# The last down projection of a two-layer trunk: the activations become the stationary operand and the weights stream, with output rows summed in the PSUM banks

## The chip, the cores and the metric

The kernel runs on one core of one Trainium2 chip. The metric is the device time of one execution in microseconds; the time before is the median of three runs. Beside it stands one execution that the hardware profiler recorded, and all rows below come from that one. Its engines are called PE (TensorE, the matmuls), PEld (the loads of PE's stationary operand), DVE (VectorE), ACT (ScalarE), POOL (GpSimd) and SP (SyncE, which here only issues DMAs).

## The reference

One step of a two-layer trunk on 512 prompt tokens and 8 x 8 sample tokens, together T = 576 tokens, with model width 1024 and a hidden width of 2816. Each layer is a mixer (a causal pool and a convolution in layer 0, a gating MLP in layer 1), and then a gated ConvFFN; each adds to the residual x. At the end stands one more RMSNorm. What matters here is the end of the last layer:

```python
def rmsnorm(x, g):
    xf = x.astype(jnp.float32)
    y = xf * lax.rsqrt(jnp.mean(xf * xf, axis=-1, keepdims=True) + EPS)
    return (y * g.astype(jnp.float32)).astype(x.dtype)
...
        h = rmsnorm(x, p["ffn_norm"][layer])
        up = h @ p["w_up"][layer]
        c, fb = causal_dwconv(up, ffn_bufs[layer], p["ffn_conv_w"][layer], p["ffn_conv_b"][layer])
        x = x + (jax.nn.silu(c[..., :D_FF]) * c[..., D_FF:]) @ p["w_down"][layer]
        new_ffn.append(fb)
    y = rmsnorm(x, p["final_norm"])
```

## The kernel before, in words

**Layout.** The kernel keeps everything transposed: features on the 128 partitions, the 576 tokens along the free dimension. The residual `X` is eight such tiles (KD = 8). A product gives one tile of 128 output features: the weights are the stationary operand (128 x 128), the activations move.

**Precision.** Each operand is split in a high part (fp32r, made by ACT with a copy) and a low part (raw minus high, made by POOL for the weights, by DVE for the activations). Each product is three matmuls: high x high, high x low, low x high. The instructions that split weights are called `split_n` (L1041 on ACT, L1664 on POOL) and, for the last projection, `last_split` (L1511 on ACT, L1935 on POOL). The four slots `w_hi[0..3]` and `w_lo[0..3]` hold 1024 columns each; `weights_at` (L127) plans which half slot a unit uses and after which unit it is free.

**The FFN in groups.** The 22 hidden tiles come in groups of 6, 6, 6 and 4. For each group the up projections, the convolution and the gating are computed, then the down projection adds the group's share to the residual. The first three groups use a scheme with fewer products. The last group has 4 hidden tiles (nt = 4) and ends the kernel: its down projection is what the change touches. Its input is `gh`, `gl` (named last_group_hi and last_group_lo in the rows), its weights are 8 tiles of 128 x 512.

**The last stage before.** The tokens are cut in two parts (`LAST`, L256): first tokens 256 to 575 (320 columns), then tokens 0 to 255. For each part PE makes eight output tiles, so there are 16 steps n, each of 4 x 3 = 12 products into bank n % 4. Steps 0 to 3 are interleaved: nine products of each, then, once the last hidden tile is there (`h_lo_ready`), the last three of each. After a step, DVE adds the residual (L2583), ACT squares the sum (L1525), ACT multiplies it by the gain of the final norm (L1533, `gained`), DVE adds the squares up (L2592), PE turns the gained tile in 128 x 128 transposes to rows (L911, `out_rows`), and DVE copies the rows to `y_rows` (L2598). At the end of a part PE sums the squares over the partitions (L634, `row_sums`), ACT takes the root (L1560), DVE the reciprocal (L2605), and the rows are scaled: those of the first part by POOL (L1974), those of the second by DVE (L2628, L2631), ACT (L1636) and POOL (L1978) together. Four DMAs from SP (L572, L574, L576) and one from ACT (L1641), of one row block of up to 128 tokens each, write them.

**What sets the order.** Each engine runs its own list in the order written, and waits on semaphores by count: `lo_ready` (a weight tile is split), `h_lo_ready` (a hidden tile is split), `acc_free` (a bank has been read), `unit_done` (a unit's products are done). Nothing is reordered by a scheduler.

Of the kernel before, what the change touches and what calls it, by code (L numbers as in the profile page):

```python
# [25 lines left out]
F32 = mybir.dt.float32  # L26
# [4 lines left out]
P = 128  # L31
# [5 lines left out]
def hybrid_trunk(nc, x, params, w_in_ab, pool_w, w_out_ab, w_in_c, w_out_c, w_up, w_down, gate_w, gate_bias,  # L37
                 gate_w_samples, pool_state, conv_state, ffn_state, state_pool, state_conv, y_prompt, y_sample,
# [96 lines left out]
    def layer_weights(u0):  # L135

        half = 0
        for g, run in enumerate(RUNS):
# [11 lines left out]
            for n in range(MS if FAST[g] else KD):  # L150
                weights_at(ud + n, half + (HALF_OF[n] if FAST[g] else 2 * n), 1 if FAST[g] else 2)
# [104 lines left out]
    LAST = (((P * 2, T), range(2, RT)), ((0, P * 2), range(2)))  # L256
# [17 lines left out]
    with ExitStack() as ctx:  # L274
# [10 lines left out]
        w_hi = [sb(f"w_hi{s}", [P, KD * P], F32R) for s in range(4)]  # L285
        w_lo = [sb(f"w_lo{s}", [P, KD * P], F32R) for s in range(4)]
# [9 lines left out]
        std = sb("std", [P, RT])  # L296
        rinv = sb("rinv", [P, RT])
# [22 lines left out]
        def cut(start, *dims):  # L320
# [5 lines left out]
            if len(dims) == 2:  # L326
# [38 lines left out]
        KL = GROUPS[-1][1] * P  # L365
        last_hi, last_lo = ([w[m][:, :] for m in range(4)]
                            + [v[:, :, :].rearrange("p k t -> p (k t)")[:, m * KL:(m + 1) * KL] for m in range(4)] for w, v in ((w_hi, xh), (w_lo, xl)))
        xg = mem[:, 0:2 * T].rearrange("p (a b) -> p a b", a=2)
# [72 lines left out]
        y_row_done, y_left, y_right = sem("y_row_done"), sem("y_left"), sem("y_right")  # L441
        xg_last, y_turned = sem("xg_last"), sem("y_turned")
        xg_ready, y_T, yrow_ready, y_scaled, st_y = sem("xg_ready"), sem("y_T"), sem("yrow_ready"), sem("y_scaled"), sem("st_y")
# [63 lines left out]
        def _(sp):  # L507
# [40 lines left out]
            for layer in range(2):  # L548
# [5 lines left out]
                for g, (t0, n) in enumerate(GROUPS):  # L554
# [12 lines left out]
                    for m in range(KD):  # L567
                        load(R_FFN[layer] + R_DOWN[g] + m, w_down[layer, m, :, t0 * P:(t0 + n) * P])
            for n, r in enumerate(LAST[0][1]):
                sp.wait_ge(y_row_done, n + 1)  # L570
                if r < CH:
                    sp.dma_start(yp_rows[:, r, :], y_rows[:, r, :]).then_inc(st_y, 16)  # L572
                else:
                    sp.dma_start(ys_rows, y_rows[P - SM:P, CH, :]).then_inc(st_y, 16)  # L574
            sp.wait_ge(y_scaled, 2)
            sp.dma_start(yp_rows[:, 0, :], y_rows[:, 0, :]).then_inc(st_y, 16)  # L576
# [6 lines left out]
            sp.wait_ge(st_y, 16 * RT)  # L583
# [3 lines left out]
        def _(pe):  # L587
# [41 lines left out]

            def row_sums(src, first=True, final=True, bank=S0, at=0, rows=range(RT)):  # L630

                for r in rows:
                    lo = r * P if r < CH else T - P
                    last = nc.tensor.matmul(PS[:, bank, at + r:at + r + 1], src[:, lo:lo + P], ones[:, 0:1],  # L634
                                            start=(first and r == rows[0]), stop=(final and r == rows[-1]),
                                            skip_group_check=True)
                return last
# [266 lines left out]
            def out_rows(n):  # L904

                pe.wait_ge(*((xg_ready, n + 1) if n < 2 * KD - 1 else (xg_last, 1)))
                if n >= 2:
                    pe.wait_ge(yrow_ready, n - 1)
                for a, r in enumerate(LAST[n // KD][1]):
                    lo = r * P if r < CH else T - P  # L910
                    last = nc.tensor.transpose(PS[:, M0 + n % 2, a * P:(a + 1) * P], xg[:, n % 2, lo:lo + P], ident[:, :])  # L911
                last.then_inc(y_T, 1)

# [75 lines left out]

            def last_products(n, ks):  # L990

                m, (lo, hi) = n % KD, LAST[n // KD][0]
# [14 lines left out]
            for n in range(4, 2 * KD):  # L1007
                if n < KD:
                    pe.wait_ge(lo_ready, ud + n + 1)
                pe.wait_ge(acc_free, ud + n - 3)  # L1010
                last_products(n, range(nt // 2))
                for q in ((0, 1) if n == 4 else (2, 3) if n == 5 else (n - 2,)):
                    out_rows(q)
                if n == KD + 1:
                    pe.wait_ge(sq_added, (KD - 1) * 4 + KD - 2)
                    row_sums(sqacc, final=False, rows=LAST[0][1])
                    pe.wait_ge(sq_ready, KD * 5)
                    row_sums(sq[:, 1, :], first=False, rows=LAST[0][1]).then_inc(var_mm, 1)
# [1787 lines left out]
```

## Time and profile before

| | |
|---|---|
| time, median of 3 runs | 1164.09 us (1163.95 to 1164.12) |
| the profiled execution: its own time | 1163.62 us |
| the profiled execution: span of its instructions | 1161.9 us |
| PE busy | 1145.3 us, 99% of the span, 8442 matmuls |
| DVE / ACT / POOL busy | 818.0 / 580.0 / 722.1 us |
| granted clock of PE, mean over the span | 0.998 |

The span runs from the first to the last instruction; the execution's own time is 1.72 us longer. Busy times of PE overlap, since matmuls are pipelined: a matmul's row starts when the one before is still draining, so what one costs is the distance between starts, not its length. The share of busy time says that PE bounds nearly the whole of the kernel; the last 42 us, which the change rewrites, are to be read from their own rows.

### The profile page before, as it was taken

The page shows a single profiled execution, that of the slowest core. Times are in us where ns is not written, and L with a number is a line of the kernel's source. Part 1 is how long each engine was busy: PE and PEld are TensorE (multiplying, and loading weights), DVE is VectorE, ACT ScalarE, POOL GpSimd, SP SyncE. Part 2 cuts the span into 40 slices and gives each one's busy share as a digit, 9 for nine tenths or more (in the row PEclk, how much of TensorE's full clock was granted, in tenths as well). Part 3 has the DMA queues.
Part 4 walks back from the last instruction along what each step waited for, and adds up shares of the span by engine and source line. Part 5 has one row for each costly group of instructions (what it writes and reads, how often), then busy time and mean ns, then how long its engine had stood idle before and what let it go on. Part 6 is the DMA issues. An engine that isn't in the chain of part 4 may idle for free. (4 is left out here: it accounts for less than half of the span.)

```text
span 1161.9 us, 21843 instructions
## 1 busy us (share of the span) xinstructions
PE 1145.3 (99%) x8442; PEld 1124.9 (97%) x8442; DVE 818.0 (70%) x1506; ACT 580.0 (50%) x1113; POOL 722.1 (62%) x691
## 2 busy tenths in 40 slices
PE   8999999999999999999999999999999999999997
PEld 8887999999999999999999999999999999999997
DVE  5999768878677867775614644388686778678655
ACT  7475555544554555453613533366346545654543
POOL 3996344359867985872564324334698679768633
PEclk9999999999999999999999999999999999999999
DMA  6311242203421422131422222322042213232312
GB/s 233 117 56 36 67 146 81 93 28 95 142 65 44 149 73 92 56 137 51 149 84 91 69 69 74 117 82 65 28 147 91 80 61 116 74 92 80 120 51 82
DMA packets 35688, 104.01 MB, mean 90 GB/s; under 512 B 5105, under 2 KB 7153, under 8 KB 35569
## 3 DMA queue, kind: packets, MB, share of 16 engines
q1 hardware_dynamic: 31504, 98.92, 26.9%
q10 hardware_dynamic: 4080, 3.69, 1.1%
q8 instruction: 67, 1.10, 0.4%
q14 instruction: 37, 0.30, 0.1%
HBM read 98.29 MB, written 4.79 MB: 89 GB/s over the span
## 5 line engine op out<-in xcount | busy, mean ns | idle before, releaser
L594 PE MATMUL psum<-x_hi,w_hi 128*128 128x320 f32 (+2 forms) x1564 | 336.4, 297 | 1.3 <-POOL w_lo L1664 1.3
L594 PE MATMUL psum<-x_lo,w_hi 128*128 128x320 f32 (+2 forms) x1564 | 334.8, 295 | 0.0
L594 PE MATMUL psum<-x_hi,w_lo 128*128 128x320 f32 (+2 forms) x1564 | 334.1, 295 | 0.0
L1664 POOL TENSOR_TENSOR w_lo<-w_raw,w_hi 128x1024 fp32r<-128x1024 f32 (+1 forms) x84 | 181.8, 2169 | 188.0 <-ACT w_hi L1041 188.0
L594 PEld LDWEIGHTS psum<-x_hi,w_hi 128*128 128x128 f32 x1564 | 258.8, 188 | 3.6 <-POOL w_lo L1664 1.6
L594 PEld LDWEIGHTS psum<-x_hi,w_lo 128*128 128x128 f32 x1564 | 258.5, 188 | 0.0
L594 PEld LDWEIGHTS psum<-x_lo,w_hi 128*128 128x128 f32 x1564 | 257.3, 188 | 0.0
L2412 DVE SCALAR_TENSOR_TENSOR psum<-arena,params,psum 128x608 f32<-128x608 f32 x176 | 150.4, 854 | 58.8 <-ACT psum L1420 55.8
L1806 POOL TENSOR_TENSOR w_lo<-arena,w_hi 128x384 fp32r<-128x384 f32 x120 | 130.8, 1109 | 49.6 <-ACT w_hi L1331 49.6
L839 PE MATMUL psum<-block_hi,w_lo 128*128 128x288 f32 x504 | 149.2, 296 | 0.0
L839 PE MATMUL psum<-block_hi,w_hi 128*128 128x288 f32 x504 | 149.2, 296 | 0.0
L839 PE MATMUL psum<-block_lo,w_hi 128*128 128x288 f32 x504 | 149.1, 296 | 0.0
L1664 POOL TENSOR_TENSOR w_lo<-arena,w_hi 128x1024 fp32r<-128x1024 f32 (+1 forms) x49 | 111.4, 2290 | 47.5 <-ACT w_hi L1041 47.5
L1420 ACT ACTIVATE psum<-arena,params 128x608 f32<-128x608 f32 x88 | 75.9, 862 | 74.1 <-DVE arena L2065 57.4
L1041 ACT ACTIVATE w_hi<-w_raw 128x1024 fp32r<-128x1024 f32 (+1 forms) x84 | 78.2, 939 | 69.0 <-PE psum L594 48.8
L1331 ACT ACTIVATE w_hi<-arena 128x384 fp32r<-128x384 f32 x120 | 58.7, 518 | 87.7 <-DVE arena L2276 28.2
L839 PEld LDWEIGHTS psum<-block_hi,w_lo 128*128 128x128 f32 x504 | 95.0, 188 | 0.0
L839 PEld LDWEIGHTS psum<-block_lo,w_hi 128*128 128x128 f32 x504 | 94.9, 188 | 0.0
L839 PEld LDWEIGHTS psum<-block_hi,w_hi 128*128 128x128 f32 x504 | 94.9, 188 | 0.0
L2290 DVE TENSOR_TENSOR residual<-psum,residual 128x288 f32<-128x288 f32 x168 | 71.7, 452 | 22.4 <-ACT squares_sum L1370 12.9
L2291 DVE TENSOR_TENSOR block_lo<-psum,block_hi 128x288 fp32r<-128x288 f32 x144 | 56.6, 415 | 20.5 <-ACT block_hi L1397 7.9
L2058 DVE TENSOR_TENSOR arena<-psum,rstd 128x512 f32<-128x512 f32 x68 | 46.7, 687 | 31.5 <-PE psum L594 31.4
(270 smaller groups left out, 2207.1 us busy)
## 6 DMA issues: line engine op xcount, KB each, us to landing
w_raw<-in_w_up SPq DMA_DIRECT2D x44, 512.0 KB, 3.7
arena<-in_w_up SPq DMA_DIRECT2D x44, 512.0 KB, 4.3
arena<-in_w_down SPq DMA_DIRECT2D x24, 384.0 KB, 3.6
w_raw<-in_w_down SPq DMA_DIRECT2D x24, 384.0 KB, 3.2
w_raw<-in_w_in_c SPq DMA_DIRECT2D x16, 512.0 KB, 3.5
w_raw<-in_w_in_ab SPq DMA_DIRECT2D x11, 512.0 KB, 3.6
w_raw<-in_w_out_ab SPq DMA_DIRECT2D x16, 256.0 KB, 2.7
w_raw<-in_w_out_c SPq DMA_DIRECT2D x8, 512.0 KB, 3.6
```

The costliest lines, as they stand in the source:

```text
L594: last = nc.tensor.matmul(PS[:, 2 * (q % 2 if slot is None else slot) + half, 0:b - a], w[q][:, k * P:(k + 1) * P], r[:, r_at, a:b], start ...
L839: last = nc.tensor.matmul(PS[:, BANK[n], 0:HALF], ws[w][:, cols + k * P:cols + (k + 1) * P], rs[:, block, k, :], start=(k == 0 and a == 0) ...
L1041: nc.scalar.activation(w_hi[slot][:, 0:nk * P], raws[RAW_SLOT[raw]][:, 0:nk * P], ACT.Copy).then_inc(hi_ready, 1)
L1331: nc.scalar.activation(w_hi[HALF_AT[ud + n] // 2][:, at:at + nk * P], src, ACT.Copy).then_inc(hi_ready, 1)
L1420: nc.scalar.activation(conv_acc(j), window(j, 0), ACT.Identity, bias=pcol("ffn_conv_b", ti + layer * 2 * KF), scale=pcol("ffn_conv_w", ti ...
L1664: nc.gpsimd.tensor_tensor(w_lo[slot][:, 0:nk * P], raws[RAW_SLOT[RAW[u]]][:, 0:nk * P], w_hi[slot][:, 0:nk * P].bitcast(F32), ALU.subtract ...
L1806: nc.gpsimd.tensor_tensor(w_lo[w][:, at:at + nk * P], src, w_hi[w][:, at:at + nk * P].bitcast(F32), ALU.subtract).then_inc(lo_ready, 1)
L2058: nc.vector.tensor_tensor(halves(dst[:, pad:pad + PR]), PS[:, 2 * slot:2 * slot + 2, 0:cut], halves(rstd[:, 0:PR]), ALU.mult)
L2290: plus = lambda out, a, b: nc.vector.tensor_tensor(out, a, b, ALU.add)
L2291: minus = lambda out, a, b: nc.vector.tensor_tensor(out, a, b, ALU.subtract)
L2412: nc.vector.scalar_tensor_tensor(out=conv_acc(j), in0=window(j, k), scalar=pcol("ffn_conv_w", ti + (layer * FK + k) * 2 * KF), in1=conv_ac ...
```

## The change

The last down projection is turned around. The activations (128 hidden features x up to 128 tokens) are the stationary operand, and the weights move, 512 columns (four output tiles) at a time. The output has tokens on the partitions, as it is to be stored. The steps are now 10: five row blocks (four of 128 prompt tokens, one of the 64 sample tokens), for the left 512 output features, and then the same five for the right. Each step begins with four transposes of the residual into the bank, and the 12 products are added on top. ACT squares the bank and sums along the row in the same instruction (`accum_out`), DVE multiplies by the gain, which now lies along the row and is loaded by one more DMA (L570 of the new kernel), and by the reciprocal root. The steps that added the residual, gained, turned back and copied are gone, and so is POOL's scaling.

For the weights to stream in one access pattern over four tiles, they all lie in `w_hi` and `w_lo` as half slots: the planner gives each of the eight tiles one half (before, the first four took a whole slot each and the others lay in the space of `x_hi`, `x_lo`). The order of the splits is unchanged on both engines.

```diff
             for n in range(MS if FAST[g] else KD):
-                weights_at(ud + n, half + (HALF_OF[n] if FAST[g] else 2 * n), 1 if FAST[g] else 2)
+                if not FAST[g] and u0 == U_FFN1:
+                    weights_at(ud + n, half + n, 1)
+                else:
+                    weights_at(ud + n, half + (HALF_OF[n] if FAST[g] else 2 * n), 1 if FAST[g] else 2)
...
-    LAST = (((P * 2, T), range(2, RT)), ((0, P * 2), range(2)))
+    LAST = [(r, h) for h in range(2) for r in range(RT)]
...
+                        if layer == 1 and g == len(GROUPS) - 1 and m == KD // 2:
+                            sp.wait_ge(unit_done, U_FFN1 + U_PAIR[RUNS[g][-1]])
+                            sp.dma_start(gain_row, final_gain.to_broadcast([P, D])).then_inc(ld_gain, 16)
...
+            for r in range(CH):
+                sp.wait_ge(y_row_done, r + 1)
+                sp.dma_start(yp_rows[:, r, :], y_rows[:, r, :]).then_inc(st_y, 16)
+            sp.wait_ge(acc_free, N_UNITS - KD + 2 * RT)
+            sp.dma_start(ys_rows[:, D // 2:D], y_rows[0:SM, CH, D // 2:D]).then_inc(st_y, 16)
...
+            def residual_rows(n):
+
+                tokens, rows, tiles = rows_of(n)
+                for a, m in enumerate(range(KD)[tiles]):
+                    nc.tensor.matmul(PS[0:rows, n % 4, a * P:(a + 1) * P], X[:, m, tokens], ident[:, :], start=(a == 0), stop=False,
+                                     is_transpose=True, skip_group_check=True)
...
-                    for a, (ws, rs) in enumerate(((last_hi, gh), (last_hi, gl), (last_lo, gh))):
-                        last = nc.tensor.matmul(PS[:, n % 4, 0:hi - lo], ws[m][:, k * P:(k + 1) * P], rs[:, k, lo:hi],
-                                                start=(k == 0 and a == 0), stop=(k == nt - 1 and a == 2))
+                    for a, (ws, rs) in enumerate(((hi_all, gh), (hi_all, gl), (lo_all, gh))):
+                        last = nc.tensor.matmul(out, rs[:, k, tokens], halves_of(ws)[:, :, k * P:(k + 1) * P],
+                                                start=False, stop=(k == nt - 1 and a == 2), skip_group_check=True)
...
             for n in range(4):
-                pe.wait_ge(lo_ready, ud + n + 1)
                 pe.wait_ge(acc_free, ud - 1 + n // 2)
-                pe.wait_ge(h_lo_ready, H_FFN[1] + nt - 1)
+                residual_rows(n)
+            pe.wait_ge(lo_ready, ud + KD // 2)
+            pe.wait_ge(h_lo_ready, H_FFN[1] + nt - 1)
+            for n in range(4):
                 last_products(n, range(nt - 1))
             pe.wait_ge(h_lo_ready, H_FFN[1] + nt)
             for n in range(4):
                 last_products(n, [nt - 1]).then_inc(unit_done, 1)
...
+            for n in range(4, 2 * RT):
                 pe.wait_ge(acc_free, ud + n - 3)
+                pe.wait_ge(y_sums, n - 3)
+                residual_rows(n)
+                if n == RT:
+                    pe.wait_ge(lo_ready, ud + KD)
+                last_products(n, range(nt)).then_inc(unit_done, 1)
...
+                for n, (r, h) in enumerate(LAST):
+                    rows = P if r < CH else SM
+                    total = row_sums[0:rows, 2 * r + h:2 * r + h + 1]
+                    act.wait_ge(unit_done, ud + n + 1)
+                    nc.scalar.activation(sq[0:rows, 0, 0:D // 2], PS[0:rows, n % 4, :], ACT.Square, accum_out=total)\
+                        .then_inc(y_sums, 1)
+                    act.wait_ge(y_sums, n + 1)
+                    if h == 0:
+                        nc.scalar.activation(row_bias[0:rows, r:r + 1], total, ACT.Identity, bias=eps[0:rows, 0:1], scale=1.0 / D)\
+                            .then_inc(y_bias, 1)
+                        continue
+                    act.wait_ge(y_bias, r + 1)
+                    nc.scalar.activation(std[0:rows, r:r + 1], total, ACT.Sqrt, bias=row_bias[0:rows, r:r + 1], scale=1.0 / D)\
+                        .then_inc(y_std, 1)
+                act.wait_ge(y_factor, RT)
+                act.wait_ge(acc_free, ud + RT)
+                left = y_rows[0:SM, CH, 0:D // 2]
+                nc.scalar.activation(left, left, ACT.Copy, scale=rinv[0:SM, CH:RT]).then_inc(y_left, 1)
+                act.wait_ge(y_left, 1)
+                act.dma_start(ys_rows[:, 0:D // 2], left).then_inc(st_y, 16)
...
+                for n, (r, h) in enumerate(LAST):
+                    rows = P if r < CH else SM
+                    cols = slice(h * D // 2, (h + 1) * D // 2)
+                    if h == 0:
+                        dve.wait_ge(y_sums, n + 1)
+                        nc.vector.tensor_tensor(y_rows[0:rows, r, cols], PS[0:rows, n % 4, :], gain_row[0:rows, cols], ALU.mult)\
+                            .then_inc(acc_free, 1)
+                        continue
+                    dve.wait_ge(y_std, r + 1)
+                    nc.vector.reciprocal(rinv[0:rows, r:r + 1], std[0:rows, r:r + 1]).then_inc(y_factor, 1)
+                    dve.wait_ge(y_factor, r + 1)
+                    nc.vector.scalar_tensor_tensor(out=y_rows[0:rows, r, cols], in0=PS[0:rows, n % 4, :], scalar=rinv[0:rows, r:r + 1],
+                                                   in1=gain_row[0:rows, cols], op0=ALU.mult, op1=ALU.mult).then_inc(acc_free, 1)
+                    if r < CH:
+                        left = y_rows[0:rows, r, 0:D // 2]
+                        dve.wait_ge(acc_free, ud + r + 1)
+                        nc.vector.tensor_scalar(left, left, rinv[0:rows, r:r + 1], None, ALU.mult).then_inc(y_row_done, 1)
```

In the rows of the order that follow, a matmul is shown as bank, moving operand, stationary operand, and the shape of what it writes; the names in brackets are the semaphores it waits for (w_lo_ready is `lo_ready` of the code). First PE where the last stage begins, in the kernel before:

```order
L995 MATMUL psum<-last_group_hi,w_hi 128x320 [waits h_lo_ready,acc_free,w_lo_ready]
L995 MATMUL psum<-last_group_lo,w_hi 128x320
L995 MATMUL psum<-last_group_hi,w_lo 128x320
...
L995 MATMUL psum<-last_group_hi,w_hi 128x320 [waits h_lo_ready]
L995 MATMUL psum<-last_group_lo,w_hi 128x320
```

Now, in the same place:

```order
L979 MATMUL psum<-ident,residual 128x128 [waits acc_free]
L979 MATMUL psum<-ident,residual 128x128 x3
...
L989 MATMUL psum<-w_hi,last_group_hi 128x512 [waits h_lo_ready,w_lo_ready]
L989 MATMUL psum<-w_hi,last_group_lo 128x512
L989 MATMUL psum<-w_lo,last_group_hi 128x512
...
L989 MATMUL psum<-w_hi,last_group_hi 128x512 [waits h_lo_ready]
L989 MATMUL psum<-w_hi,last_group_lo 128x512
```

Before, the first product waits for the first weight tile alone and the transposes come later; now 16 transposes stand ahead, and the first product waits for the first four weight tiles. The two rows with the wait for h_lo_ready alone begin the last hidden tile's products of the first four steps.

The end of DVE's list, before:

```order
L2583 TENSOR_TENSOR residual<-psum,residual 128x256 [waits unit_done]
L2621 TENSOR_SCALAR arena<-residual,params 128x256 [waits y_T,acc_free]
L2598 COPY arena<-psum 128x2x128 [waits y_T]
L2605 RECIPROCAL rinv<-std 128x2 [waits std_ready]
L2628 TENSOR_SCALAR arena<-psum,rinv 128x128 [waits y_T,rinv_ready]
L2628 TENSOR_SCALAR arena<-psum,rinv 128x128
L2631 TENSOR_SCALAR arena<-arena,rinv 128x896 [waits yrow_ready]
```

And now:

```order
L2523 RECIPROCAL rinv<-std 128x1 [waits y_std]
L2525 SCALAR_TENSOR_TENSOR arena<-psum,rinv,arena 128x512 [waits y_factor]
L2530 TENSOR_SCALAR arena<-arena,rinv 128x512 [waits acc_free]
L2523 RECIPROCAL rinv<-std 64x1 [waits y_std]
L2525 SCALAR_TENSOR_TENSOR arena<-psum,rinv,arena 64x512 [waits y_factor]
```

Of the seven instructions behind the last product two are left on DVE, and the rows of the step before are finished before them.

## Rows read from the trace of the kernel before

**Rows 1.** Stretches of the last stage: us, busy us (x instructions), PE clock, DMA share, GB/s

```profile
1120.10:1124.10 4.00, 4.00 (x30) 3.89 (x28) 2.65 (x5) 1.94 (x3) 1.62 (x4) 1.00 0.24 66
1129.30:1134.10 4.80, 3.59 (x27) 2.96 (x25) 3.60 (x8) 2.86 (x8) 2.23 (x2) 1.00 0.00 0
...
1154.10:1161.90 7.80, 1.39 (x12) 1.06 (x10) 2.46 (x7) 1.40 (x3) 3.24 (x2) 0.75 0.62 223
...
1157.00:1158.00 1.00, 0.00 (x0) 0.00 (x0) 0.35 (x1) 0.00 (x0) 0.71 (x1) 0.99 0.95 205
1158.00:1159.00 1.00, 0.00 (x0) 0.00 (x0) 0.00 (x0) 0.00 (x0) 0.00 (x0) 0.50 0.96 328
```

**Rows 2.** Chain of waits, its end: start us, us, what

```profile
1147.35 7.93 POOL arena L1974 x3
1155.28 0.88 issue
```

**Rows 3.** Timeline of PE, last stage: start us, us, instruction [idle before, releaser]

```profile
1120.11 0.31 PE L995 MATMUL psum<-last_group_hi,w_hi 128*128 128x320 f32 x1
...
1123.92 0.31 PE L995 MATMUL psum<-last_group_hi,w_lo 128*128 128x320 f32 x1
1124.08 0.41 PE L995 MATMUL psum<-last_group_hi,w_hi 128*128 128x320 f32 x1
1124.34 0.31 PE L995 MATMUL psum<-last_group_lo,w_hi 128*128 128x320 f32 x1
...
1126.57 0.41 PE L995 MATMUL psum<-last_group_hi,w_hi 128*128 128x320 f32 x1 [0.90 <-DVE last_group_lo L2291]
...
1139.88 0.49 PE L911 MATMUL psum<-ident,arena 128*128 128x128 f32 x3
...
1140.33 0.28 PE L995 MATMUL psum<-last_group_lo,w_hi 128*128 128x256 f32 x1
...
1141.50 0.28 PE L995 MATMUL psum<-last_group_hi,w_lo 128*128 128x256 f32 x1
...
1153.76 0.28 PE L995 MATMUL psum<-last_group_hi,x_lo 128*128 128x256 f32 x1
...
1155.48 0.42 PE L911 MATMUL psum<-ident,arena 128*128 128x128 f32 x2
```

**Rows 4.** Timeline of PE in the convolution: nine products of 512 columns

```profile
49.48 4.02 PE L739 MATMUL psum<-arena 128*128 128x512 f32 x9
```

**Rows 5.** Timeline of POOL: the fourth weight tile's split

```profile
1122.73 1.30 POOL L1935 TENSOR_TENSOR w_lo<-arena,w_hi 128x512 fp32r<-128x512 f32 x1 [1.25 <-ACT w_hi L1511]
```

**Rows 6.** Timeline of DVE, ACT and the DMA issues behind the last product

```profile
1154.08 0.42 DVE L2583 TENSOR_TENSOR residual<-psum,residual 128x256 f32<-128x256 f32 x1
...
1155.65 0.26 ACT L1560 ACTIVATE std<-psum,eps 128x2 f32<-128x2 f32 x1 [0.70 <-PE psum L634]
1155.95 0.17 DVE L2605 RECIPROCAL rinv<-std 128x2 f32<-128x2 f32 x1 [0.72 <-ACT std L1560]
1156.15 0.61 DVE L2628 TENSOR_SCALAR arena<-psum,rinv 128x128 f32<-128x128 f32 x2
...
1157.82 0.34 ACTq L1641 DMA_DIRECT2D out_y_prompt<-arena  x1
```

**Rows 7.** Groups by line and shape: busy us, mean ns of one

```profile
L1592 ACT ACTIVATE arena<-psum 128x512 f32<-128x512 f32 x8 | 4.7, 590 | 4.3 <-PE psum L935 4.3
...
L2145 DVE SCALAR_TENSOR_TENSOR psum<-arena,params,psum 128x512 f32<-128x512 f32 x85 | 57.4, 752 | 0.0
L2058 DVE TENSOR_TENSOR arena<-psum,rstd 128x512 f32<-128x512 f32 x68 | 46.7, 687 | 31.5 <-PE psum L594 31.4
```

**Rows 8.** DMA issues: KB each, median us to landing

```profile
out_sgu_v_prompt<-arena ACTq DMA_DIRECT2D x8, 64.0 KB, 1.6
out_y_prompt<-arena ACTq DMA_DIRECT2D x1, 512.0 KB, 3.6
...
out_y_sample<-arena SPq DMA_DIRECT2D x1, 256.0 KB, 3.0
```

More of the change, by code:

```diff
@@ L284, in hybrid_trunk @@
         w_raw = [sb(f"w_raw{s}", [P, KD * P]) for s in range(2)]
-        w_hi = [sb(f"w_hi{s}", [P, KD * P], F32R) for s in range(4)]
-        w_lo = [sb(f"w_lo{s}", [P, KD * P], F32R) for s in range(4)]
+        hi_all, lo_all = sb("w_hi", [P, 4, KD * P], F32R), sb("w_lo", [P, 4, KD * P], F32R)
+        w_hi, w_lo = ([w[:, s, :] for s in range(4)] for w in (hi_all, lo_all))
         par = sb("params", [P, NPAR])
@@ L364, in hybrid_trunk @@
         u2 = back_raw[:, 0, :]
[L365 to L368, printed above, removed]
+        gain_row = mem[:, 0:D]
         y_rows = mem[:, 2 * T:2 * T + RT * D].rearrange("p (a b) -> p a b", a=RT)
@@ L628, in two_units @@
                     products(HALF_AT[u + q] // 2, nk - 1, nk - 1, nk, rh, rl, False, True, q).then_inc(unit_done, 1)
[L630 to L637, printed above, removed]
             def spread(r):
@@ L902, in ffn @@
                             unit(q, ud + 4 + q, nt, gh, gl)
[L904 to L912, printed above, removed]
             ffn(0)
@@ L1006, in _ @@
                 last_products(n, [nt - 1]).then_inc(unit_done, 1)
-            for n in range(4, 2 * KD):
-                if n < KD:
-                    pe.wait_ge(lo_ready, ud + n + 1)
+            for n in range(4, 2 * RT):
                 pe.wait_ge(acc_free, ud + n - 3)
[L1011 to L1018, printed above, removed]
-                last_products(n, range(nt // 2, nt)).then_inc(unit_done, 1)
-            out_rows(2 * KD - 2)
-            pe.wait_ge(sq_added, (KD - 1) * 4 + 2 * (KD - 2))
-            row_sums(sqacc, final=False, bank=S1, rows=LAST[1][1])
-            pe.wait_ge(sq_ready, KD * 6)
-            row_sums(sq[:, 1, :], first=False, bank=S1, rows=LAST[1][1]).then_inc(var_mm, 1)
-            out_rows(2 * KD - 1)
+                pe.wait_ge(y_sums, n - 3)
[3 more added lines that the diff above has]
+                last_products(n, range(nt)).then_inc(unit_done, 1)
         @block.scalar
@@ L1040, in split_n @@
                     act.wait_ge(unit_done, BUFFER_FREE[u])
-                nc.scalar.activation(w_hi[slot][:, 0:nk * P], raws[RAW_SLOT[raw]][:, 0:nk * P], ACT.Copy).then_inc(hi_ready, 1)
+                at = HALF_AT[u] % 2 * (KD // 2 * P)
+                nc.scalar.activation(w_hi[slot][:, at:at + nk * P], raws[RAW_SLOT[raw]][:, 0:nk * P], ACT.Copy)\
+                    .then_inc(hi_ready, 1)
             def norm_in(n, m, r, gname, gi):
@@ L1555, in last_stage @@
-                last_root(1, S1)
-            def last_root(part, bank):
-                act.wait_ge(var_mm, 7 + part)
-                a, b = LAST[part][1][0], LAST[part][1][-1] + 1
-                nc.scalar.activation(std[:, a:b], PS[:, bank, a:b], ACT.Sqrt, bias=eps[:, 0:1], scale=1.0 / D)\
-                    .then_inc(std_ready, 1)
+                split_n(ud + 7)
+                for n, (r, h) in enumerate(LAST):
[12 more added lines that the diff above has]
+                        .then_inc(y_std, 1)
@@ L2595, in take_rows @@
-                def take_rows(n):
-                    m, rows = n % KD, LAST[n // KD][1]
-                    dve.wait_ge(y_T, n + 1)
-                    nc.vector.tensor_copy(y_rows[:, rows[0]:rows[-1] + 1, m * P:(m + 1) * P],
-                                          PS[:, M0 + n % 2, 0:len(rows) * P].rearrange("p (r c) -> p r c", c=P))\
-                        .then_inc(yrow_ready, 1)
-                def last_factors(part):
-                    a, b = LAST[part][1][0], LAST[part][1][-1] + 1
-                    dve.wait_ge(std_ready, 7 + part)
-                    nc.vector.reciprocal(rinv[:, a:b], std[:, a:b]).then_inc(rinv_ready, 1)
@@ L2607, in last_stage @@
-                for n in range(2 * KD - 1):
-                    for q in (() if n < 4 else (0, 1) if n == 4 else (2, 3) if n == 5 else (n - 2,)):
-                        take_rows(q)
-                    last_residual(n)
-                    if n % KD not in (0, KD - 1):
-                        last_square(n)
-                    if n == KD + 2:
-                        last_factors(0)
-                n = 2 * KD - 1
-                take_rows(n - 2)
-                last_residual(n)
-                lo, hi = LAST[1][0]
```

133 lines of the change are left out of this document (22 added, 111 removed).

## The prediction, as put on record before the changed kernel was run

> **What bounds the kernel now.** I read the stretches first, then PE's timeline, then the end of the chain of waits, since the change lies wholly in the last 42 us. From 1120.10 to 1124.10 PE is full at clock 1.00; behind the last product it does almost nothing for 7.8 us [rows 1]. So there are two parts with different limits. Up to 1153.88, where the last product's slot ends (its start at 1153.76 and 0.12), PE sets the time [rows 3]. Behind it is a tail: residual, square, sums, root, reciprocal, scaling, DMA. The chain of waits runs in that tail through POOL's scaling of the first part's rows until 1155.28 [rows 2], but that is only the chain that this view picks; the second part's own path (1154.08 residual, 1155.65 root, 1155.95 reciprocal, last DMA at 1157.82) is later [rows 6], and it is the one that must become shorter. The last DMA takes 3.6 us to land [rows 8], at 1161.42, and the span ends 0.48 us later.
>
> **PE's part.** *Price of a product.* Twenty-six starts from 1120.11 to 1123.92 give 146.5 ns for 320 columns, ten from 1140.33 to 1141.50 give 117 ns for 256 [rows 3]. At 2.4 GHz 320 columns are 133.3 ns, so 13 ns are left over; 512 columns are then 226.6 ns. In proportion to the columns it is 234.4 ns. I take 229, a third of the way, as the two steps of size that I have leave a leftover that grows slowly. The weights now stream in four pieces of 128 columns from four places, which no row shows; I price it at nothing, and a rival has the other case.
>
> *Price of the transposes.* Three of them, with the 256-column product behind, take 1139.88 to 1140.33, 0.45 us; less the product, 0.33. That is 0.11 each and includes the slower start of the product. Four are 0.45 us [rows 3].
>
> *The start.* Before, products begin at 1120.11, wait for the fourth weight tile at 1124.08 (POOL is done with it at 1124.03 [rows 5]), and stand still 0.90 us until 1126.57, for the last hidden tile [rows 3]. After, the first product waits for all four tiles, and the order of the splits does not change: it starts at 1124.08. In front of it are 16 transposes, 1.8 us, of which eight wait for the last up unit's banks to be read; they are hidden in the 4.0 us, of which they fill less than half. So this wait costs about 4 us of PE, less the 1.8 us of transposes that are done in it, and the 0.90 us stall goes, as 36 products of 0.229 last until 1132.4, long past 1126.57. The gain row's DMA and the shifted load behind it are issued when the last up pair begins, two units ahead of the stage; I cost them at nothing. With the last four weight tiles it is the same: they are needed only at step 5.
>
> *The sum.* Start 1124.08, +0.11 (the first of a series is later: 1124.08 to 1124.34 against 0.147 [rows 3]), +48 x 0.229 = 10.99: steps 0 to 3 end at 1135.18. Six more steps of 12 x 0.229 + 0.45 = 3.20 us: 1154.37. Before it was 1153.88. The change takes out 72 products (192 to 120), but the columns go up from 96 x 320 + 96 x 256 = 55,296 to 120 x 512 = 61,440, since the 64 sample tokens stream the weights as if they were 128; it is a small loss, and PE's part gives nothing.
>
> *Do the banks hold PE up?* Step 4 needs the bank of step 0. That ends at 1124.19 + 39 x 0.229 = 1133.12, +0.20; then a square, 0.74 as worked out below, and a multiplication by the gain, 0.69 [rows 7]: 1134.8, with 0.4 us to spare before 1135.18. Later steps have 3.2 us for some 1.1 us of ACT and 1.4 of DVE: hidden.
>
> **The tail.** From the slot's end to the first reader 0.20 us, as before (1153.88 to 1154.08 [rows 6]): 1154.57. ACT squares 64 x 512 from PSUM: 0.59 for such a read [rows 7], plus 0.15 for the sum along the row. No row shows that sum; it is between nothing and 0.30, a little over the 0.26 of a small ACT instruction [rows 6]: 1155.31. Root: 0.03 handing over and 0.30 until the reciprocal starts (1155.65 to 1155.95): 1155.64. Until the next DVE instruction 0.20 (1155.95 to 1156.15 [rows 6]): 1155.84. The multiplication by factor and gain 0.75 [rows 7]: 1156.59, issue at 1156.62. ACT's half of the sample rows, 0.7 us from the same reciprocal, is issued together with it. Each of the two DMAs carries 128 KB. The nearest rows are 64 KB in 1.6 us and 256 KB in 3.0 [rows 8]; I take 2.1: 1158.72. The 512 KB of the row block before are issued at about 1153.9 (3.2 us earlier plus a scaling of 0.5) and, at 3.6 us, land by 1157.5: hidden. With 0.48 as before the span ends at 1159.2, against 1161.9: -2.7 us. The profiled execution would take 1163.62 - 2.7 = 1160.9; the runs' median lies 0.47 above that execution, so I forecast 1161.4.
>
> **What the forecast's own range is.** Low: products at 226.6 ns (-0.3), no cost of the sum (-0.15), DMA 1.6 (-0.5): 1160.4. High: 234.4 ns (+0.65), 0.30 for the sum (+0.15), DMA 3.0 (+0.9): 1163.1.
>
> **Rivals.**
>
> *The clock falls at the start (slower).* Between 1120.1 and 1124.08 PE has 16 transposes and 2 us of nothing, then its densest work. What speaks for a fall: after its last instruction, ended at 1155.90 [rows 3], the granted clock was at 1.2 GHz from 1158.00 on, 2.1 us later [rows 1]. Against it: with 1.2 us idle and the twelve transposes of out_rows 0 to 3 between 1129.30 and 1134.10 the clock stayed at 1.00 [rows 1]. The Trainium skill says in "TensorE: Matmul & The Clock Gate", part 4 (PE-mode transpose), that transposes do not count as PE being busy in the same way. By that rule the new stretch counts as idle for 4.0 us, twice the 2.1 us above, and the clock falls; if transposes count as products do, the idle time is 2.0 us, and it need not. At 1.2 GHz a product takes 213 ns more. The forecast's 2.7 us are gone after 13 products; the kernel is slower beyond what can be told after 24; through all 36 of the first block it is +7.7: 1169.1. A short dip of eight products is +1.7: 1163.1. No row shows how long a dip lasts.
>
> *The tail gives less.* The sum along the row is an instruction of its own on ACT, the handing over to the next ACT instruction costs more than 0.03, and two DMAs at once take 3.0: together +1.3 us, 1162.7. For it: no row has an ACT instruction that waits for its own predecessor's sum. Against: the tail has four links where before it had seven.
>
> *The wide products are slow (slower).* Nine products of 512 columns in the convolution start 0.43 us apart ((4.02 - 0.59) / 8) [rows 4]. Those are plain fp32 operands, these are fp32r like the 320-column ones, so I hold it unlikely. If it were so: 120 x 0.2 = +24: 1185. If only the four pieces cost something, 10 ns each, it is +3.6: 1165.0.
>
> **Chances.** Forecast 0.56, less from the tail 0.20, clock 0.17 (0.10 short, 0.07 long), slow products 0.07. What a measurement of this kernel can tell from no change is about 0.2%, 2.3 us, that is below 1161.8 or above 1166.4. Of the forecast's 0.56 some 0.45 lie below 1161.8, with 0.02 of the tail's case: faster 0.47. Long clock and slow products beyond 1166.4: slower 0.11. The rest is same: 0.42. The range: 1160.3 to 1164.0 leaves out the long dip and the slow products, 0.12, and the edges.
>
> **What would show it.** In the new profile: the first product at about 1124.1, starts 229 ns apart, no idle time of PE before 1154.4, granted clock 1.00 from 1120 to 1154, ACT's squares 0.6 to 0.75 us, the last DMA issued 2.2 to 2.5 us behind the last product. I am wrong if PE waits for y_sums or acc_free at a step's start, if the clock shows 0.50 behind 1122, or if the last landing is over 3 us behind its issue.

## The result, and the profile after

The changed kernel takes 1167.95 us (median of 7 runs, 1166.73 to 1168.92), the kernel before, run beside it, 1164.09 us (7 runs, 1163.80 to 1164.44). The ratio is 1.0032, 95% interval [1.0022, 1.0042]: slower by 0.3%, where 1161.4 was forecast. The profiled execution took 1166.81 us, its span is 1164.8 us (before 1163.62 and 1161.9).

**The stage itself.** PE's timeline where the last stage begins, and around its first sample-token step and its end; the columns are start us, us, instruction, and in brackets the idle time before it and its releaser:

```profile
1124.34 0.43 PE L594 MATMUL psum<-x_hi,w_lo 128*128 128x256 f32 x2
1124.61 2.24 PE L979 MATMUL psum<-ident,residual 128*128 128x128 f32 x16
1128.55 0.50 PE L989 MATMUL psum<-w_hi,last_group_hi 128*128 128x512 f32 x1 [1.70 <-POOL w_lo L1613]
1128.89 0.40 PE L989 MATMUL psum<-w_hi,last_group_lo 128*128 128x512 f32 x1
1129.12 0.39 PE L989 MATMUL psum<-w_lo,last_group_hi 128*128 128x512 f32 x1
...
1139.62 0.39 PE L989 MATMUL psum<-w_lo,last_group_hi 128*128 128x512 f32 x1
1139.86 0.60 PE L979 MATMUL psum<-ident,residual 128*64 128x128 f32 x4
1140.21 0.47 PE L989 MATMUL psum<-w_hi,last_group_hi 128*64 128x512 f32 x1
...
1158.95 0.40 PE L989 MATMUL psum<-w_lo,last_group_hi 128*64 128x512 f32 x1
```

Three things are to be seen. The first product starts 3.94 us behind the first transpose, with 1.70 us of waiting for the fourth weight tile; the forecast had 1124.08 - 1120.11 = 3.97 [rows 3]. The products and transposes after it show no idle time, so neither the banks nor the last hidden tile hold PE up. But the whole starts at 1124.61, and before it was 1120.11 [rows 3]: 4.5 us are already lost when the first rewritten instruction of the stage runs.

The last link, first the chain of waits behind the last products (start us, us, what), then the two DMA issues of the sample rows from the timeline, then the same two DMAs in the list of issues (KB each, us to landing):

```profile
1158.88 0.48 PE psum L989 x2
1159.36 0.02 issue
1159.38 0.03 ACT squares L1503
1159.41 0.47 issue
1159.88 0.20 ACT squares L1503
1160.07 0.02 issue
1160.10 0.30 ACT std L1511
1160.40 0.02 issue
1160.42 0.17 DVE rinv L2523
1160.59 0.02 issue
1160.62 0.74 DVE arena L2525
```

```profile
1161.37 0.50 ACTq L1518 DMA_DIRECT2D out_y_sample<-arena  x1
1161.39 0.53 SPq L576 DMA_DIRECT2D out_y_sample<-arena  x1
```

```profile
out_y_sample<-arena ACTq DMA_DIRECT2D x1, 128.0 KB, 2.3
out_y_sample<-arena SPq DMA_DIRECT2D x1, 128.0 KB, 2.9
```

The square with its row sum lasts from 1159.38 to 1160.07 and the root starts at 1160.10, so 0.72 us (forecast 0.74). The last issue comes 2.21 us behind the end of the last product's slot (1158.95 + 0.233), as forecast (2.25). The later of the two landings takes 2.9 us instead of 2.1.

From the first transpose to the span's end the stage takes 1164.8 - 1124.61 = 40.2 us; the kernel before took 1161.9 - 1120.11 = 41.8 for the same, and the forecast was 1159.2 - 1120.11 = 39.1. The rewrite gains 1.6 us instead of 2.7.

**The 4.5 us ahead of it.** They must come from work that the change does not touch. Ahead of the last stage both traces have the same 8190 matmuls, so they can be lined up one by one from the start. They run together up to 170 us, within 0.3 us; then the changed kernel is 1.25 us late at 260 us, 1.6 at 480, 2.2 from 560 to 740, 3.6 at 940, 4.2 at 1100 and 4.5 at the stage. Summed by line and shape, the distances from one start to the next grow by 5.5 us in the pairs of 320- and 256-column products at L594 (3.7 and 1.8), where PE waits for nothing. The other lines together give 1.0 us back, 0.9 of it in the 672 products of 288 columns at L870, whose moving operands also lie in the arena; e1, e3 and e11, at the same place, show the same 0.9. The stretch from 200 to 240 us, PE at L594 alone (length, busy us with the number of matmuls, granted clock, DMA share, GB/s), of the kernel before:

```profile
200.00:240.00 40.00, 40.00 (x305) 1.00 0.27 83
```

and of the changed one:

```profile
200.00:240.00 40.00, 40.00 (x300) 1.00 0.26 78
```

Both are full and both have clock 1.00, but the second gets 300 products done where the first does 305. The timeline shows it without a count; each of these rows is a pair, one product of 320 and one of 256 columns. Before:

```profile
199.84 0.43 PE L594 MATMUL psum<-x_lo,w_hi 128*128 128x256 f32 x2
...
202.75 0.42 PE L594 MATMUL psum<-x_hi,w_hi 128*128 128x256 f32 x2
```

Changed:

```profile
199.98 0.43 PE L594 MATMUL psum<-x_hi,w_hi 128*128 128x256 f32 x2
...
202.66 0.43 PE L594 MATMUL psum<-x_lo,w_hi 128*128 128x256 f32 x2
```

Before, the two starts are eleven pairs apart, 264.5 ns a pair; now ten pairs, 268 ns. From the start of a 320-column product to the next start it is 146.1 ns before and 148.9 now, as a mean over the 40 us, and for 256 columns 118.3 and 119.4. These distances are no scatter: they come in a pattern that repeats over the whole 40 us with deviations of at most 1 ns, before every six starts (118, 148, 118, 144, 120, 146 ns), now every eight (149, 118, 145, 117, 150, 125, 152, 118). The page hints at it in the mean durations of L594: 298, 296 and 296 ns, where they were 297, 295 and 295. That is 3 ns in 146, in instructions that are the same in both programs.

What could reach them is where their operands lie. The new kernel has 8 columns less in `params` (-32 bytes per partition) and two small buffers ahead of the arena, `row_sums` of 10 floats (64 bytes with rounding) and `row_bias` of 5 (32 bytes). The arena starts with `x_hi` and `x_lo`, the moving operand of these products. It began at byte 78880 of a partition and now begins at 78944, 64 bytes on. Below, "mod 128" is what is left of such an address when it is divided by 128: 32 before, 96 now.

### The profile page after: what moved, and what is told of

It reads as the page before. It is cut to its first block and busy times, and to the rows that moved or that the text cites. A ratio compares the mean times of both kernels' runs of the same rounds, so it can differ in the third digit from the quotient of the medians.

```text
span 1164.8 us, 21575 instructions
## 1 busy us (share of the span) xinstructions
PE 1149.8 (99%) x8350; PEld 1123.1 (96%) x8350; DVE 808.6 (69%) x1476; ACT 575.5 (49%) x1110; POOL 715.2 (61%) x687
## 5 line engine op out<-in xcount | busy, mean ns | idle before, releaser
L594 PE MATMUL psum<-x_hi,w_hi 128*128 128x320 f32 (+2 forms) x1564 | 339.1, 298 | 1.3 <-POOL w_lo L1613 1.3
L594 PE MATMUL psum<-x_lo,w_hi 128*128 128x320 f32 (+2 forms) x1564 | 336.0, 296 | 0.0
L594 PE MATMUL psum<-x_hi,w_lo 128*128 128x320 f32 (+2 forms) x1564 | 335.9, 296 | 0.0
L594 PEld LDWEIGHTS psum<-x_hi,w_hi 128*128 128x128 f32 x1564 | 259.8, 188 | 3.6 <-POOL w_lo L1613 1.6
L594 PEld LDWEIGHTS psum<-x_hi,w_lo 128*128 128x128 f32 x1564 | 260.0, 188 | 0.0
L594 PEld LDWEIGHTS psum<-x_lo,w_hi 128*128 128x128 f32 x1564 | 260.0, 188 | 0.0
L830 PE MATMUL psum<-block_hi,w_lo 128*128 128x288 f32 x504 | 148.9, 295 | 0.0
L1613 POOL TENSOR_TENSOR w_lo<-arena,w_hi 128x1024 fp32r<-128x1024 f32 (+1 forms) x52 | 116.6, 2261 | 49.5 <-ACT w_hi L1026 49.4
L2223 DVE TENSOR_TENSOR residual<-psum,residual 128x288 f32<-128x288 f32 x168 | 71.7, 452 | 23.5 <-ACT squares_sum L1356 13.2
```

Of the source, the lines that this page charges most:

```text
L594: last = nc.tensor.matmul(PS[:, 2 * (q % 2 if slot is None else slot) + half, 0:b - a], w[q][:, k * P:(k + 1) * P], r[:, r_at, a:b], start ...
L830: last = nc.tensor.matmul(PS[:, BANK[n], 0:HALF], ws[w][:, cols + k * P:cols + (k + 1) * P], rs[:, block, k, :], start=(k == 0 and a == 0) ...
L1613: nc.gpsimd.tensor_tensor(w_lo[slot][:, at:at + nk * P], raws[RAW_SLOT[RAW[u]]][:, 0:nk * P], w_hi[slot][:, at:at + nk * P].bitcast(F32), ...
L2223: plus = lambda out, a, b: nc.vector.tensor_tensor(out, a, b, ALU.add)
```

## The experiments

Theory A in the expectations is that address; A1 says that the place of `x_hi`, `x_lo` itself counts, A2 that of some other buffer of the arena; B puts the loss on the new code; C says that the granted clock dips in the 3.94 us ahead of the first product, which would explain why the runs of the changed kernel fall in a lower group (1166.73 to 1166.81) and an upper one (1167.95 to 1168.92); D that the upper group has another cause. The table has all twelve, with the 320-column spacing of 200 to 240 us; every ratio is to the kernel before, run on the same chip in the same batch (1163.95, 1163.79 and 1163.98 us for e1 to e4, e5 to e8, e9 to e12).

| | x_hi at byte | median us (range, runs) | ratio [95%] | 320-column spacing, ns |
|---|---|---|---|---|
| e1 before, arena + 64 B | 78944 | 1168.59 (1168.43 to 1168.74, 5) | 1.0041 [1.0027, 1.0055] | 149.0 |
| e2 changed, at its old place mod 1024 | 79904 | 1162.22 (1161.93 to 1164.01, 11) | 0.9988 [0.9979, 0.9997] | 146.1 |
| e3 changed, early split | 78944 | 1164.84 (1164.60 to 1164.97, 11) | 1.0008 [0.9999, 1.0017] | 149.0 |
| e4 e2 and e3 together | 79904 | 1160.40 (1160.22 to 1160.79, 7) | 0.9971 [0.9960, 0.9983] | 146.1 |
| e5 before, all but x + 64 B | 78880 | 1163.07 (1162.65 to 1163.33, 10) | 0.9994 [0.9984, 1.0003] | 146.1 |
| e6 before, x + 64 B, the rest at its place mod 1024 | 78944 | 1169.05 (1168.54 to 1169.52, 4) | 1.0046 [1.0029, 1.0062] | 148.9 |
| e7 before, 0 mod 128 | 78976 | 1165.75 (1165.05 to 1167.16, 10) | 1.0016 [1.0007, 1.0026] | 149.3 |
| e8 before, 64 mod 128 | 78912 | 1157.73 (1157.41 to 1157.95, 4) | 0.9948 [0.9931, 0.9964] | 145.3 |
| e9 changed, 64 mod 128 | 79936 | 1156.03 (1155.97 to 1157.42, 4) | 0.9934 [0.9918, 0.9949] | 145.4 |
| e10 e9 with early split | 79936 | 1153.81 (1153.73 to 1154.50, 4) | 0.9912 [0.9897, 0.9928] | 145.5 |
| e11 changed, the wait filled with products | 78944 | 1166.81 (1166.18 to 1167.11, 11) | 1.0022 [1.0013, 1.0031] | 149.0 |
| e12 e10, 64 mod 128 but another 256 | 79040 | 1152.17 (1151.26 to 1152.36, 4) | 0.9897 [0.9882, 0.9912] | 143.4 |

**e1 and e2: the address by itself, both ways.** One unused buffer ahead of the arena, in the kernel before (e1, 16 floats) and in the changed one (e2, 240 floats):

```diff
+        pad_columns = sb("pad_columns", [P, 16])
         ARENA = 18788
```

> The kernel before with one unused buffer of 16 floats put ahead of the arena, so that x_hi, x_lo, h_hi, h_lo and all else in the arena lie where the changed kernel has them (78944 bytes from the partition's start instead of 78880). Nothing else is changed. Theory A (the 4.5 us that the changed kernel loses ahead of its last stage come from the place of the moving operand in SBUF): the 320-column products of L594 start 149 ns apart instead of 146, the last stage begins 4 to 5 us later, the time is 1168.0 to 1169.0. Theory B (they come from the new code: the planner, the gain's DMA, the longer or shorter instruction stream): the time is as before, 1164.1, within 0.5.

> The changed kernel with one unused buffer of 240 floats ahead of the arena, so that the arena lies 1024 bytes behind its place in the kernel before: the same place modulo 64, 128, 256, 512 and 1024 bytes. Theory A: the last stage begins at about 1120.1 again; the stage itself stays at 40.2 us against 41.8 before, so that the fastest runs take 1162.3 to 1162.8, with runs 1.5 us higher among them if the clock falls in the wait ahead of the first product. Theory B: no change, 1166.7 to 1168.9.

e1 has not one changed instruction and loses 4.6 us; the same stretch of its trace, from 200 to 240 us, in the same columns:

```profile
200.00:240.00 40.00, 40.00 (x300) 1.00 0.24 75
```

e2, the new code at the old place modulo 1024, has the 305 back, begins its stage within 0.2 us of where the kernel before did, and is 0.12% faster than it:

```profile
200.00:240.00 40.00, 40.00 (x305) 1.00 0.26 83
```

```profile
1120.28 2.24 PE L980 MATMUL psum<-ident,residual 128*128 128x128 f32 x16
1124.21 0.50 PE L990 MATMUL psum<-w_hi,last_group_hi 128*128 128x512 f32 x1 [1.70 <-POOL w_lo L1614]
...
1154.70 0.40 PE L990 MATMUL psum<-w_lo,last_group_hi 128*64 128x512 f32 x1
```

This is the picture that the forecast drew (1120.11, 1124.08, 1154.14). Theory A holds and B falls: all but 0.2 of the 4.5 us go with the address.

**e5 and e6: which buffer.** A gap between `x_lo` and the rest of the arena moves the one without the other (16 floats in e5; 240 floats, and 16 ahead, in e6):

```diff
-        whole = sb("arena", [P, 2 * HIDDEN + ARENA])
-        mem = whole[:, HIDDEN:2 * HIDDEN + ARENA]
+        GAP = 16
+        whole = sb("arena", [P, 2 * HIDDEN + GAP + ARENA])
+        mem = whole[:, HIDDEN + GAP:2 * HIDDEN + GAP + ARENA]
...
-            return nc.alloc_sbuf_tensor_at(name, [P, *dims], F32R, offset=at + 4 * start)
+            return nc.alloc_sbuf_tensor_at(name, [P, *dims], F32R, offset=at + 4 * (start + (GAP if start >= HIDDEN else 0)))
```

> The kernel before with 64 unused bytes between x_lo and the rest of the arena: x_hi and x_lo, the moving operand of the up projections (L594), stay where they are, everything behind them (h_hi, h_lo, blocks, taps, the third and fourth raw buffer) moves by 64 bytes. Theory A1 (the place of the moving operand itself sets the distance between the products' starts): 1164.0, and 320-column products 146 ns apart. Theory A2 (another buffer of the arena does, by what DVE, ACT, POOL or the DMAs do to the same memory meanwhile): 1168.5, 149 ns.

> The kernel before with x_hi and x_lo 64 bytes further on and everything behind them 1024 bytes further on. Theory A1: 1168.5 and 149 ns for the 320-column products of L594. Theory A2: 1164.0 and 146 ns. If both parts count, something between in both this and the kernel with the gap behind x_lo.

e5 keeps its speed and is even 0.7 us below the kernel before, which its interval does not quite tell from nothing; e6 loses 5.3 us and has 301 products in the stretch:

```profile
200.00:240.00 40.00, 40.00 (x301) 1.00 0.27 81
```

So A1: the loss goes with the place of the moving operand itself. It is not quite the only thing that counts. In e5, where x_hi and x_lo did not move, the long stretches of pairs keep their 146.1 and 118.3 ns, but four shorter ones of 96 pairs each change to 147.0 to 147.2 and 116.2 to 116.4 (the first is at 340 us), and L870 is 0.7 us quicker in all.

**e7 and e8: the other two places.** The kernel before with 24 and with 8 floats of padding.

> The kernel before with the arena 96 bytes further on, at a multiple of 128 bytes (before: 32 above one; changed kernel: 96 above one). If only the place within 128 bytes counts and an even place is best, 1164.0 or less; if the order of cost goes with the distance from the old place, 1168.5 or more. I have no theory that says which; 1162 to 1170.

> The kernel before with the arena 32 bytes further on, 64 above a multiple of 128. The fourth of the places that the allocation's step of 32 bytes allows within 128. As for the place at a multiple of 128: 1162 to 1170, and the lowest of the four tells where the changed kernel should be put.

e8 came out far below what was expected of it (1162 to 1170). By place within 128 bytes the kernel before takes 1157.7 us (64), 1163.8 (32), 1165.75 (0) and 1168.6 (96): 0.9% from best to worst with not one instruction changed. The kernel before did not stand at its best place, and the change moved it to the worst of the four. At 64 the 288-column products are quicker too: 132.2 ns apart instead of 133.3. They make up most of what e8 gains ahead of the last stage: of 6.1 us, 2.5 come from them at L594 and 1.4 at L839, and 1.7 from the pairs. The moving operands of L839, `block_hi` and `block_lo`, lie in the arena as well, and e7 and e8 move all of it.

**e3, e4: the wait ahead of the first product.** The fourth weight tile of the last stage is split right behind the third on ACT and POOL, instead of behind the two up units that follow; on POOL:

```diff
+                                if layer == 1 and not FAST[g] and i == GROUPS[g][1] - 1 and j == 1:
+                                    split_n(ud + 3)
...
-                    for m in range(3, KD + (0 if layer else 3)):
+                    for m in range(4 if layer else 3, KD + (0 if layer else 3)):
```

> The changed kernel, with the split of the fourth weight tile of the last projection (ACT's copy and POOL's subtraction) put right behind that of the third, ahead of the last tap instruction, in layer 1 only. PE's wait for it (1.7 us idle between the 16 transposes and the first product) should go: the first product starts about 2.4 us behind the stage's begin instead of 3.9, and the time falls by 1.5 us at least. If the runs of the changed kernel lie in two groups (1166.7 and 1168.2) because the clock falls in that wait in some of them (theory C), the runs of this one lie together within 0.5 us at 1165.2. If the two groups have another cause (theory D), they stay, 1.5 us apart.

> Both edits of the two kernels before on the changed kernel: the arena moved by 960 bytes and the fourth split early. With theories A and C: 1160.7 to 1161.2, all runs within 0.5 us. With B: as the early split alone.

PE's timeline of e4 at the stage's begin shows the wait gone:

```profile
1120.24 2.24 PE L980 MATMUL psum<-ident,residual 128*128 128x128 f32 x16
1122.24 0.48 PE L990 MATMUL psum<-w_hi,last_group_hi 128*128 128x512 f32 x1
```

The first product comes 1.97 us earlier than in e2, and the median falls by 1.8 us (1162.22 to 1160.40). The range shrinks as well: none of the 11 runs of e3 and 7 of e4 lies more than 0.6 us above the lowest. Both medians are 0.3 to 0.4 us below what was expected of them.

**e11: the same wait, filled.** Seven products whose results are overwritten, ahead of the transposes:

```diff
+            pe.wait_ge(acc_free, ud - 1)
+            pe.wait_ge(h_lo_ready, H_FFN[1] + 1)
+            for _ in range(7):
+                nc.tensor.matmul(PS[:, 0, :], gh[:, 0, 0:P], xh[:, 0, 0:PSUM_BANK], start=True, stop=True)
```

> The changed kernel, at its own place, with seven products of 512 columns ahead of the 16 transposes (the results are overwritten, so they only keep PE busy while it would wait for the fourth weight tile). They last 7 x 0.233 = 1.6 us of the 1.7 us idle, so the first real product starts as before. Theory C (the upper group of the changed kernel's runs, 1168.0 to 1168.9, is a fall of PE's clock in that wait): all runs in the lower group, 1166.6 to 1167.1, and no clock of 0.997. Theory D (the upper group has another cause, such as the longer time that the stage's reads and DMAs take in some runs): about half of the runs above 1167.9, as for the changed kernel.

```profile
1124.99 1.77 PE L996 MATMUL psum<-x_hi,last_group_hi 128*128 128x512 f32 x7
1126.60 1.91 PE L979 MATMUL psum<-ident,residual 128*128 128x128 f32 x16
1128.94 0.50 PE L989 MATMUL psum<-w_hi,last_group_hi 128*128 128x512 f32 x1 [0.43 <-POOL w_lo L1617]
```

PE still waits for the weight tile, and starts the real products 0.4 us later than the changed kernel, but all 11 runs lie between 1166.18 and 1167.11 us, at a mean clock of 0.999 (once 1.000), as theory C has it; by D about half should have been above 1167.9. Of the changed kernel's seven, three lie at 1168.26 to 1168.92 us with a mean clock of 0.997 or 0.998 and spans of 1166.5 to 1167.0; the other four have 0.999 or 1.000 and spans of 1164.8 to 1165.3 (one of them, 1167.95, is high because of time outside its span). Such runs with 0.997 are seen again where the wait stands, 2 of 11 in e2 and 1 of 4 in e9, each 1.2 us or more above the rest: 6 of 22 in all. There is none in the 37 runs in which the wait is gone or filled (e3, e4, e10, e11, e12). The kernel before, with its shorter waits, has 2 in 57, and its five moved versions 1 in 33.

So the wait costs its 2 us in every run (1166.8 to 1164.84 from the changed kernel's lower group to e3, 1162.2 to 1160.4 from e2 to e4), and in some runs about 1.5 us come on top. That these are a dip of the clock is inferred. The mean clock of a run is lowered by its end too: in every profiled execution the clock is 1.00 from 7.2 us on until the last product, and it falls to 0.50 behind it, 1.6 us (e5) to 5.1 us (e9) after the last matmul has ended. In the changed kernel the last matmul ends 5.4 us before the span does, so by these figures the end lowers the mean by at most (5.4 - 1.6) / 2 / 1165 = 0.0016, to 0.998; 0.997 needs more time at 0.50 elsewhere. A dip of 3 us at 0.50 does 1.5 us of work too little and lowers the mean by 0.0013, which fits. No profiled execution shows the dip itself; what speaks for it are these means and that the upper group is absent once the wait is filled or gone. The Trainium skill says in "TensorE: Matmul & The Clock Gate", part 4 (PE-mode transpose), that transposes do not count as PE being busy in the same way. That the 16 transposes and the wait together had such runs, and with products ahead or without the wait had none, is in line with it; but no run has the same wait without transposes, so it is not shown.

**e9, e10, e12: the parts put together.** The changed kernel with 248 floats of padding (e9), the same with the early split (e10), and the early split with 24 floats (e12).

> The changed kernel with 248 unused floats ahead of the arena, so that it lies 64 bytes above a multiple of 128, and at the same place modulo 1024 as in the fastest of the moved kernels before (1157.7). Theory A1: the place of x and the rewriting of the last stage are separate and add up. Then it is 1157.7 less the 1.6 to 1.8 us that the last stage gives at equal places: 1155.9 to 1156.2 for most runs, a few of them 1.6 higher. If the two are not separate (the stage's own products of 512 columns gain or lose by the place as well), it lies outside 1155 to 1157.5.

> As the kernel before this, with the fourth weight tile split early. The early split was worth 1.8 us at the place of the kernel before (1162.2 to 1160.4), and took the spread away: 1154.0 to 1154.6, all runs within 0.6 us. It would be the fastest, by 9.7 us against the kernel before.

> As the changed kernel with early split and the arena 64 above a multiple of 128, but with 24 instead of 248 floats, so 64 above a multiple of 128 and 192 (not 64) above a multiple of 256. If only the place within 128 bytes counts: as its sister, 1154.0 to 1154.6. If the place within 256 or more counts too: between that and 1160.4.

At the good place the change is worth 1.7 us again (e8 to e9, in two batches, so by the medians alone: the intervals of the two ratios overlap) and the early split 2.2 (e9 to e10, in one batch). e12 stands at 64 mod 128 like e10 but 1.6 us lower, below both ranges that were expected of it, with the densest stretch of all (200 to 240 us):

```profile
200.00:240.00 40.00, 40.00 (x310) 1.00 0.31 89
```

So more than the place within 128 bytes counts: e10 lies at 64 mod 256, e12 at 192. e12, at 1152.17 us, is the fastest kernel here: ratio 0.9897 to the kernel before, 11.8 us, of which the rewrite and the early split give 3.5 to 4 and the rest is the place.

## Why the prediction was wrong

- **"The change lies wholly in the last 42 us."** This is the step that failed. Nothing in the sum stood for the products ahead of the stage, since their instructions are the same. But the diff's new buffers and the shorter `params` move the arena by 64 bytes, and at the new place the 320-column product costs 148.9 ns instead of 146.1. The missing term is +4.5 us (5.5 in the pairs, less 1.0 elsewhere); e1 shows it without the change, e2 the change without it. No rival of the prediction named it. The forecast at unchanged places was 1161.4, and e2 came to 1162.2.
- **The price of a product:** 229 ns taken, 233.3 measured (46 starts from 1128.89 to 1139.62). With 120 products that is +0.5, of which slightly cheaper transposes (0.42 us a step, not 0.45) take 0.2 back: from the first transpose to the last slot's end 34.57 us against 34.26. The upper bound, in proportion to the columns (234.4), was the nearer one. The prediction's own two sizes said so: what is left over grows from 10.3 ns at 256 columns to 13.2 at 320, and in a straight line that gives 235 ns at 512; "grows slowly" was a misreading.
- **The start:** right, 3.94 us against 3.97, no stall for the last hidden tile.
- **Banks:** right, no idle time of PE between 1128.55 and 1159.2.
- **The tail:** the links up to the issue are right (2.21 against 2.25 us). The row sum is an instruction of its own (the section on the change has it in the same instruction), as that rival said, but costs 0.2 us in all. The landing is the mis-sized term: 2.9 against 2.1, near the row of 256 KB in 3.0 [rows 8], and 2.9 or 3.0 in every profile of the new code. Half the bytes twice at once landed no sooner than all of them once.
- **Rivals:** the clock did not fall in the stage of the profiled execution; in three of the seven runs (mean clock 0.997, 0.997, 0.998) a short dip is likely, at about the price given for it (+1.7). The 2.1 us from the last matmul to the fall, against which the prediction held the new wait, is not a fixed figure: over the profiles it is 1.6 to 5.1. Wide products are not slow: 0.456 ns a column, where the 320-column ones have 0.457 to 0.465.
- **From the profiled execution to the median:** 1.14 us where 0.47 was taken. The median is the run of 1167.95, whose clock (1.000) and span (1165.3) belong to the lower group and which spent 2.6 us outside its span instead of 1.7 to 2.0; with three higher and three lower runs it stands in the middle by chance. The lower group alone (1166.8) would have missed the forecast too.
- **Together:** -2.7 forecast, +0.3 for PE, +0.8 for the landing give -1.6; +4.5 gives +2.9 for the span, as measured (1161.9 to 1164.8); 0.3 more outside the span (2.0 against 1.7) and 0.7 more from the profiled execution to the median (1.14 against 0.47) give the +3.9 of the medians.

What stays open is why the place matters: for the move of 64 bytes it is the moving operand's address (e5, e6); at the other places, where the whole arena moved, each step of 32 bytes counts, and not the place within 128 bytes alone. A rival is that other engines or DMAs touch the same part of the memory at the same time. The traces speak against it, since the distances between starts repeat to within 2 ns over 40 us in every profile (every six starts before, every eight in the changed kernel, every four in e12), while DVE, ACT and POOL work at other intervals (66, 44 and 22 instructions beside the 305 products of the kernel before); but no experiment isolates it, and what inside the read makes the pattern is not shown.

## What to carry to other kernels

A change that adds or drops a small buffer moves every buffer behind it; compare the operands' addresses of the two programs before you compare their code, and where PE is full, time the new code once with padding that puts them back. Then time the kernel at several paddings: here the best place was worth more than three times the rewrite (6.1 us, e8, against 1.7). And when a stage opens with transposes and a wait, move the wait's source ahead, even if the wait is short: in 6 of 22 runs here it cost more than its length.

## What the runs showed of the hardware

- The spacing of fp32r products with PE full and clock 1.00 depends on where the moving operand begins in SBUF: 143.4 (e12), 145.3 (e8), 146.1 (before), 149.0 (e1) and 149.3 ns (e7) for 320 columns; over the whole kernel 0.9% at equal code. The single distances repeat in a fixed pattern.
- ACT's `accum_out` is a second instruction: 0.19 us, with the first together 0.72 for 64 x 512 from PSUM, until ACT's next instruction starts.
- Behind the last matmul the granted clock fell to 0.50 after 1.6 us in one profile (e5) and after 5.1 in another (e9).
- Two DMAs of 128 KB from SBUF issued 0.02 us apart by ACT and SP landed after 2.3 and 2.9 us.
- Sixteen transposes of 128 x 128 fp32 are followed by a product without a gap, 2.0 us behind the first transpose (e4).
